# Two half slabs of the modulation moved forward in the first attention unit, and weight chunks split ahead of the first activation of a gate-up loop

## The reference

```
# block 1: x (256 x 1024), ctx (256 x 1024), one vector c
mod = silu(c) @ w_ada + b_ada                  # 1024 x 6144; six parts: sh_m, sc_m, gt_m, sh_f, sc_f, gt_f
px  = (rms_norm(x)   * (1 + sc_m) + sh_m) @ w_in       # queries, keys, values, mLSTM inputs, gates
pc  = (rms_norm(ctx) * (1 + csc_m) + csh_m) @ w_in
att = softmax(q k^T, banded + context keys + sink) v   # 8 heads, 256 queries, 512 keys
ml  = bidirectional mLSTM in chunks                    # its forget gates are summed along the tokens
x   = x + gt_m * rms_norm(concat(att, ml) @ w_out)
h   = rms_norm(x) * (1 + sc_f) + sh_f
x   = x + gt_f * rms_norm((silu(h @ w_gate) * (h @ w_up)) @ w_down)     # hidden width 2816
# block 2: SwiGLU, attention with sinks + gated linear attention, SwiGLU, final norm
```

## Time and profile before

| | |
|---|---|
| median of 3 timed runs | 1023.13 us (1020.88 to 1025.48) |
| the profiled execution's own time | 1014.95 us |
| its span, first to last instruction | 1013.2 us |
| granted TensorE clock over the span (1 is full) | 0.988 |
| PE busy | 977.3 us, 96% |
| DVE busy | 657.0 us, 65% |
| ACT busy | 498.4 us, 49% |

### The profile page before, as it was taken

One profiled execution on the slowest core, in us unless ns is written; L12 is line 12 of the kernel. 1 busy time (PEld: TensorE's weight loads), 2 busy tenths in 40 slices (PEclk: granted clock), 3 DMA queues, 4 the chain that ended last, 5 costly groups with the idle time before them and its releaser, 6 DMA issues.

```text
span 1013.2 us, 19459 instructions
## 1 busy us (share of the span) xinstructions
PE 977.3 (96%) x7547; PEld 910.4 (90%) x7547; DVE 657.0 (65%) x1008; ACT 498.4 (49%) x774; POOL 75.4 (7%) x101
## 2 busy tenths in 40 slices
PE   4998999999999999999999999999999999999996
PEld 2776777989999999899999999998888999999995
DVE  4788887577666765765555555754966775565553
ACT  3664546654545543554445334644545555444530
POOL 0102012110000021000000012000210100000000
PEclk8999998999999999999999999999999999999998
DMA  9953346456656794165556736542433556666841
GB/s 349 385 175 126 116 134 215 144 173 189 194 168 189 194 299 152 62 214 175 166 176 189 219 104 196 167 144 64 125 109 121 169 166 207 187 184 199 218 122 41
DMA packets 189439, 175.41 MB, mean 173 GB/s; under 512 B 7344, under 2 KB 178624, under 8 KB 189008
## 3 DMA queue, kind: packets, MB, share of 16 engines
q1 hardware_dynamic: 183888, 154.29, 49.8%
q0 software_dynamic: 4928, 17.51, 5.0%
q10 hardware_dynamic: 576, 2.97, 0.7%
HBM read 173.67 MB, written 1.05 MB: 172 GB/s over the span
## 4 chain that ended last, share of the span: by engine, by line
PE 86%; DVE 8%; ACT 3%; issue 2%; DMA 1%; SPq 0%; DVEq 0%; ACTq 0%
PE acc L1962 22%; PE acc L1963 22%; PE acc L1964 22%; PE acc L2348 2%; DVE lo L1128 2%; PE wk L2400 1%; PE acc L2152 1%; DMA slab_hi<-in_w_ada 1%; PE acc L2153 1%; PE acc L2154 1%; ACT hi L600 1%; DVE inv L1182 1%; PE wk L2616 1%; PE wk L1962 1%; PE wk L1964 1%
## 5 line engine op out<-in xcount | busy, mean ns | idle before, releaser
L1128 DVE TENSOR_TENSOR lo<-raw,hi 128x1024 fp32r<-128x1024 f32 (+1 forms) x260 | 333.7, 1296 | 199.9 <-ACT hi L600 199.5
L600 ACT ACTIVATE hi<-raw 128x1024 fp32r<-128x1024 f32 (+1 forms) x260 | 282.9, 1098 | 132.2 <-PE acc L1964 123.7
L1962 PE MATMUL acc<-nH,hi 128*128 128x272 f32 (+3 forms) x1016 | 291.2, 287 | 2.9 <-DVE gab L1920 1.1
L1963 PE MATMUL acc<-nL,hi 128*128 128x272 f32 (+3 forms) x1016 | 289.7, 285 | 0.0
L1964 PE MATMUL acc<-nH,lo 128*128 128x272 f32 (+3 forms) x1016 | 288.7, 284 | 0.0
L1962 PEld LDWEIGHTS acc<-nH,hi 128*128 128x128 f32 (+1 forms) x1016 | 191.4, 188 | 5.4 <-DVE lo L1128 2.1
L1963 PEld LDWEIGHTS acc<-nL,hi 128*128 128x128 f32 (+1 forms) x1016 | 191.0, 188 | 0.4
L1964 PEld LDWEIGHTS acc<-nH,lo 128*128 128x128 f32 (+1 forms) x1016 | 190.9, 188 | 0.2
L1962 PE MATMUL acc<-gH,hi 128*128 128x256 f32 (+1 forms) x528 | 149.5, 283 | 0.8 <-DVE lo L1128 0.8
L1964 PE MATMUL acc<-gH,lo 128*128 128x256 f32 (+1 forms) x528 | 149.2, 283 | 0.0
L1963 PE MATMUL acc<-gL,hi 128*128 128x256 f32 (+1 forms) x528 | 149.0, 282 | 0.0
(11 more groups left out here) (421 smaller groups left out, 1307.9 us busy)
## 6 DMA issues: line engine op xcount, KB each, us to landing
raw<-in_w_in SPq DMA_DIRECT2D x52, 512.0 KB, 3.6
raw<-in_w_ffn_in SPq DMA_DIRECT2D x44, 512.0 KB, 4.4
raw<-in_ffn_w_gate SPq DMA_DIRECT2D x44, 512.0 KB, 3.6
raw<-in_ffn_w_up SPq DMA_DIRECT2D x44, 512.0 KB, 3.6
raw<-in_ffn_w_down SPq DMA_DIRECT2D x32, 704.0 KB, 4.8
stage<-in_w_ada POOLq DMA_DIRECT2D x24, 512.0 KB, 5.5
raw<-in_w_ffn_out SPq DMA_DIRECT2D x16, 704.0 KB, 6.5
raw<-in_w_out SPq DMA_DIRECT2D x16, 512.0 KB, 3.4
```

The costliest lines, as they stand in the source:

```text
L600: act.activation(hi[:, j, 0:width], raw[:, j, 0:width], ACT.Copy).then_inc(hi_ready, 1)
L1128: dve.tensor_tensor(lo[:, j, 0:width], raw[:, j, 0:width], hi[:, j, 0:width].bitcast(F32), ALU.subtract).then_inc(lo_ready, 1)
L1962: pe.matmul(out_, wH, xH, start=start, stop=False)
L1963: pe.matmul(out_, wH, xL, start=False, stop=False)
```

## The change

Three edits. In the first attention unit the product of half slab 2 comes ahead of the wait for the gates' logarithm, and the product of half slab 3 moves from the end of unit 1 to the end of unit 0. POOL's load of half slab 3 moves ahead of its wait for the same gates. In the first gate-up loop (`shifted=True`) ACT makes all three splits of the second group ahead of its first silu, and DVE puts the split of chunk 3 between the multiplication of up and gate and the wait for ACT's rounded copy. Nothing is added or removed, and no matmul moves.

```
@@ gpsimd
             stage_half(2, 1)
+            stage_half(3, 2)
             pool.wait_ge(glog_ready, 2)
             for d in range(2):
                 pool.dma_start(MR[:, d, :], glog[8 * d + 4:8 * d + 8, :]).then_inc(rows_in, 16)
                 pool.dma_start(rR[:, d, :], gt[8 * d:8 * d + 4, :]).then_inc(rows_in, 16)
-            stage_half(3, 2)
@@ scalar, pipeline(..., shifted=False)
-                if silu:
+                if silu and shifted:
+                    for j in (1, 2, 3):
+                        split(first + 1, j, width)
+                    evac(0, 1)
+                    evac(0, 3)
+                elif silu:
                     split(first + 1, 1, width)
                     evac(0, 1)
@@ vector, pipeline(..., shifted=False)
                     split(first + 1, 2, width)
-                    evac(0, 3)
-                    split(first + 1, 3, width)
+                    if shifted:
+                        evac(0, 3, lambda: split(first + 1, 3, width))
+                    else:
+                        evac(0, 3)
+                        split(first + 1, 3, width)
@@ vector, units
                 if n == 0:
                     rope(4)
+                    slab_product(2)
                     dve.wait_ge(glog_ready, 1)
...
-                if n in (0, 1, 5, 6):
-                    slab_product({0: 2, 1: 3, 5: 5, 6: 6}[n])
+                if n in (0, 5, 6):
+                    slab_product({0: 3, 5: 5, 6: 6}[n])
@@ vector, gate_up_shifted
                         ins.then_inc(hb_ready, 1)
+                        if meanwhile:
+                            meanwhile()
                         dve.wait_ge(gh_ready, i + 1)
```

More of the change, by code:

```diff
@@ L600, in split, with pipeline @@
                 act.activation(hi[:, j, 0:width], raw[:, j, 0:width], ACT.Copy).then_inc(hi_ready, 1)
-            def pipeline(name, width, evac, ahead, evac_first=False, silu=False, behind=((0,), (1,), (2,), (3,)), between=None):
+            def pipeline(name, width, evac, ahead, evac_first=False, silu=False, behind=((0,), (1,), (2,), (3,)), between=None,
+                         shifted=False):
                 first, n = BASE[name], COUNT[name]
-                if silu:
+                if silu and shifted:
[4 more added lines that the diff above has]
+                elif silu:
                     split(first + 1, 1, width)
@@ L903, in evac @@
                         act.activation(gH[:, ds(2 * i, 2), 0:T], hbuf[:, :, 0:T], ACT.Copy).then_inc(gh_ready, 1)
-                pipeline(name, 1024, evac, ahead, silu=True, behind=((0,), (1,), (), (2, 3)))
+                pipeline(name, 1024, evac, ahead, silu=True, behind=((0,), (1,), (), (2, 3)), shifted=True)
             def gate_up_scaled(name, f, width, ahead):
@@ L1129, in split, with pipeline @@
                                   ALU.subtract).then_inc(lo_ready, 1)
-            def pipeline(name, width, evac, ahead, evac_first=False, peel=False, behind=((0,), (1,), (2,), (3,)), between=None):
+            def pipeline(name, width, evac, ahead, evac_first=False, peel=False, behind=((0,), (1,), (2,), (3,)), between=None,
+                         shifted=False):
                 first, n = BASE[name], COUNT[name]
@@ L1668, in gate_up_shifted, with evac @@
             def gate_up_shifted(name, ahead):
-                def evac(i, j):
+                def evac(i, j, meanwhile=None):
                     if j == 1:
@@ L1689, in evac @@
                                           gH[:, ds(2 * i, 2), 0:T].bitcast(F32), ALU.subtract).then_inc(gl_ready, 1)
-                pipeline(name, 1024, evac, ahead, peel=True, behind=((0,), (), (), (1, 2, 3)))
+                pipeline(name, 1024, evac, ahead, peel=True, behind=((0,), (), (), (1, 2, 3)), shifted=True)
             def evac_half(name, width, t0):
```

## The result

In thirteen executions of each kernel the changed kernel took 1010.91 us (median; 1009.09 to 1017.43) and the kernel before 1021.01 us (1015.72 to 1025.62). The profiled execution of the changed kernel took 1010.46 us (span 1008.7, mean granted clock 0.988), where that of before took 1014.95 (span 1013.2, 0.988). So two figures stand side by side from the first: the profiles differ by 4.5 us, the medians by 10.1. Most of what follows is about that gap.

A forecast was written before the change was run, and what follows sets the result against it. PE was taken as the bound, waiting for DVE in attention unit 2 and gate-up, with a clock loss behind. Attention 4.4 plus gate-up 1.7 gives 6.1 us off 1023.13: 1017.0, range 1013.5 to 1021.

The forecast's parts named there:

- The waits: PE's waits at attention unit 2's transposes and the second gate-up group: removing them gives 2.7 and 1.7 us.
- half 2 in the idle stretch: DVE, first attention unit: half slab 2's 2.87 us fill the 2.76 us idle before the gates' logarithm, gates 0.1 later.
- half 3 in its place: DVE: half slab 3 takes half 2's old place, 0.27 us longer; unit 2's maxima start at 91.03, before 93.90.
- the loads hidden: POOL's two moved 512 KB loads of half slab 3 cost nothing, covered by a gap of 1.9 us.
- the silu in time: ACT at gate-up: silu ends at 227.8, 0.6 us later than before, yet ahead of DVE's L1684 at 228.2.
- The wait foreseen as the next at unit 3's transposes: Unit 3's second normalised tile reaches PE with only 0.1 us to spare, the next wait to appear.
- The clock: From unit 2's transposes to unit 3's scores PE runs at full clock, 3.76 us instead of 5.54: gain 1.8 us.
- both waits go, but the clock gives nothing: Rival, chance 0.22: 1.7 us are off the sum, leaving a gain of 4.4 us, 1018.7.
- clock 1.00 from 86 to 120: Sign that the forecast is right: PE's granted clock stays full through this window of the first attention unit.
- The later low stretch changes: Rival, chance 0.08: the low-clock stretch around 162 us gets shorter or longer, moving the end 1 to 1.5 us.
- a new wait in units 3 or 4: Rival, chance 0.12: DVE or ACT late at unit 3's second tile; attention gives only 2.4 us, total 1019.0.
- I take 6.1 off it as well: The whole gain of 6.1 us, derived from the profiled execution, subtracted from the timed median 1023.13 to give 1017.0.

The follow-up runs named there:

- att_only: Kernel before with only POOL's and DVE's new order of the half slabs in attention; 1015.53 us, ratio 0.9954.
- after_look2: The changed kernel, unchanged, in one further profiled execution; 1008.57 us.
- after_spread: Changed kernel with unit 3's gate columns moved on PE behind the transposes of the probabilities; 1012.33 us, ratio 0.9933.
- base_fill: Kernel before with twelve unused products of 512 columns where PE waited in unit 2; 1020.61 us, ratio 0.9995.
- gu_only: Kernel before with only the gate-up edits, ACT's shifted order and DVE's moved split of chunk 3; 1016.38 us, ratio 0.9983.
- half2_only: Kernel before with only half slab 2's product moved ahead of the wait for the gates; 1016.69 us, ratio 0.9976.
- after_spread2: Same as after_spread, with the last chunk of the gates also behind the first context states; 1011.97 us, ratio 0.9929.
- base_look6: The kernel before, unchanged, in one further profiled execution; 1020.39 us.

## Why the prediction was wrong

**The waits: right.** The forecast of 2.7 us for the attention and 1.7 for the gate-up, 4.4 together, measures 4.7; the halves alone give 2.6 and 1.6. Every step of it (half 2 in the idle stretch, half 3 in its place, the loads hidden, both gate-up waits gone, the silu in time) is in the rows above. The wait foreseen as the next at unit 3's transposes did not appear, not even where the clock did not fall (`att_only`, transposes at 105.70; `after_look2`, 105.46), and showed at 0.56 us in `after_spread`, where PE came to them at 104.7.

**The clock: right in kind, mis-sized.** The term was the 1.8 us (1.7 in the sum) that the clock cost between the transposes of unit 2 and the scores of unit 3, from one execution. The stretch that it prices was there in seven profiles of seven with the wait and in none of ten without it, and `base_fill` shows that PE's idleness brings it about, with the wait for DVE left in place. What the term left out is all the later falls, which it put at nothing. In four of its other five profiled executions the kernel before had a second low stretch in unit 3 or 4, which the first profile did not have. Over the six, the low time in 95 to 115 is 5.7 us on average; over the four of the changed kernel 0.9. That is 2.4 us of time. Of the other kernels, `gu_only`, which keeps the wait, had 6.8 us there; `att_only`, `half2_only`, `after_spread` and `after_spread2` had none, and `base_fill`, which fills the wait, had 3.4 and none. So seven executions of seven with PE idle for 2.9 us fell there, and two of ten with that idleness gone or shortened. The rival *both waits go, but the clock gives nothing* describes the one execution that was profiled first, where the forecast's sign "clock 1.00 from 86 to 120" failed; in the other three of the changed kernel it held. *The later low stretch changes* came true beside the forecast, and nothing of a late chunk, a new wait in units 3 or 4, or a late silu was seen in the changed kernel.

**What stands against that as the whole story.** Behind unit 4 the low time in 155 to 175 rose from 6.8 to 8.5 us, which takes 0.9 back, and at 670 to 710 it fell from 5.7 to 2.6, which gives 1.6. Together 2.4 - 0.9 + 1.6 = 3.1 us, and 4.7 + 3.1 = 7.8. The timed executions agree: the mean of all of before is 1020.2 us (97, error 0.3), of the changed kernel 1011.9 (28, error 0.5), a difference of 8.3 with an error of 0.6; and the mean granted clock, 0.9854 against 0.9887 over the 84 and 28 of them for which it is listed, makes 0.0033 x 1013 = 3.3 us of it, a rough figure, since the clock of executions like `base_look6` lacks the opening. The rounds ran on four chips and more; the mean of before lies between 1019.3 and 1021.2 us in each of the four timed sets, that of the changed kernel between 1011.8 and 1012.7 in its three, so the chip does not make the difference. Executions more than 7.8 us above the lowest of their kernel, which in the two profiles of before at 1023 are those with the long stretch at 692, are 31 of 97 before and 2 of 28 after. The change touches nothing near 692, where PE only comes 4.5 us earlier. Why the clock falls there less often stays open, and so does how much of the gain in units 3 and 4 is owed to the wait and how much to PE's coming earlier; with six and four profiles the three shares are rough, and that `base_fill` gained at most a little in the mean shows that a stretch avoided in one place can come back in another.

**The median of three.** The step "I take 6.1 off it as well" failed most plainly: the gain was taken off a median of three that was no measure of the kernel. The three runs of before (1023.13, 1020.88, 1025.48) came from executions that lie in groups near 1015.8, 1018.4, 1021, 1023.7 and 1025.4 us; the mean of all 97 is 1020.2. The miss of 6.1 us adds up: 2.9 from a median that stood above the mean, 2.2 from a gain of 8.3 and not 6.1 (0.3 of it in the waits, 4.7 for 4.4, and 1.9 in the clock, 3.6 for 1.7), and 1.0 from a median of after that lies below its own mean (1011.9). The prediction's range gave the median two us of movement; among sets of three drawn from the 97, one in five has a median of 1023 or more, and the profiled execution, 8.2 us lower and with its own clock of 0.988, was the sign that it was such a set. The range does not follow from its own terms either: its upper end should be 1023.1 - 2.4 + 2 = 1022.7 and not 1021; the lower end is right (1023.1 - 7.5 - 2 = 1013.6), and there the result fell out.

## What to carry to other kernels

When the timed runs of a kernel lie 1% apart, profile it two or three times before pricing anything: list where the clock falls in each execution, and compare time less half of the low time, which here told a difference of 2 us apart in single executions, as long as their openings were alike. A wait of PE cost its own length in every execution here, and the low stretch right behind it too; the later ones came and went, so price them from several executions. And subtract a forecast from a mean that is known, not from the median of three runs.

## What was not expected of the hardware

- The granted clock fell while PE was busy in every window: in unit 3 behind 14 products of 4 rows and 8 of one column (the rows at 100.83 to 101.89; in `att_only` and `after_look2` it stayed at 1.00 behind the same products), and at 692 us in two executions of before behind products of 64 rows and 64 columns (L2558 and L2560, 688.6 to 693.7), for 13.7 us with PE busy 2.00 of 2.00. In the other four executions of before the clock stood at 1.00 behind the same products; two of them had 3.4 us of low clock at 681 to 687.
- Executions of one program with the same waits of PE took 1014.95 to 1023.13 us, and in five of the six profiled the difference is half of the low time within 0.8 us; the sixth has 2.1 us more, from its opening.
- Twelve unused products in the place of an idle stretch of 2.9 us took away the low stretch behind it in two profiles of two (3.97 us for work that took 5.54), and the mean of the timed runs did not fall.
- A table load with work queued on both sides cost ACT 1.28 us and about 0.03 us more (at 222.97 in the first profile of the changed kernel).
